# W2 block sums in the opening block, a reordered seam of the MLP products, and the last four tiles by column halves

## The reference

```python
def _mlp(h, w1, b1, w2, b2):
    return jnp.square(jax.nn.relu(h @ w1 + b1)) @ w2 + b2
...
        pl = jnp.split(hl @ w_in[l] + b_in[l], PROJ_SPLITS, axis=-1)
        ...
        hl2 = _modulate(xl, mod_l[3], mod_l[4])
        xl = _layernorm(DEEPNORM_ALPHA * xl + mod_l[5] * _mlp(hl2, w_mlp1[l], b_mlp1[l], w_mlp2[l], b_mlp2[l]),
                        ln_post_g[l, 1], ln_post_b[l, 1])
```

## Time and profile before

| | us |
|---|---|
| median of 3 runs (lowest to highest) | 3223.57 (3222.33 to 3227.64) |
| the profiled execution's own time | 3226.03 |
| its span, first to last instruction | 3224.2 |
| TensorE busy | 2957.7 (92%) |
| VectorE busy | 1853.1 (57%) |
| ScalarE busy | 1033.3 (32%) |
| GpSimd busy | 482.0 (15%) |
| mean granted TensorE clock, share of full | 0.965 |

### The profile page before, as it was taken

One profiled execution on the slowest core, in us unless ns is written; L12 is line 12 of the kernel. 1 busy time (PEld: TensorE's weight loads), 2 busy tenths in 40 slices (PEclk: granted clock), 3 DMA queues, 4 the chain that ended last, 5 costly groups with the idle time before them and its releaser, 6 DMA issues.

```text
span 3224.2 us, 35999 instructions
## 1 busy us (share of the span) xinstructions
PE 2957.7 (92%) x13816; PEld 2428.7 (75%) x13816; DVE 1853.1 (57%) x2496; ACT 1033.3 (32%) x1676; POOL 482.0 (15%) x628
## 2 busy tenths in 40 slices
PE   6999999999996889989999798897999799989994
PEld 3888888888884678868788576775888688878883
DVE  5831133112222878857766766665777666687667
ACT  2421000111112555542112444444555433313330
POOL 0423011010101222202202200010111000060003
PEclk9999999999999999989999898898999899999997
DMA  6732233333334545448847666776888755545552
GB/s 227 250 116 82 76 104 121 114 113 106 127 112 154 176 132 177 135 140 236 230 158 245 233 203 199 209 249 216 252 266 262 251 211 189 189 160 212 194 184 98
DMA packets 332912, 573.01 MB, mean 178 GB/s; under 512 B 23731, under 2 KB 212419, under 8 KB 326726
## 3 DMA queue, kind: packets, MB, share of 16 engines
q1 hardware_dynamic: 256646, 330.00, 32.1%
q0 software_dynamic: 58128, 200.85, 18.6%
q10 hardware_dynamic: 17968, 39.85, 3.7%
HBM read 371.37 MB, written 199.24 MB: 177 GB/s over the span
## 4 chain that ended last, share of the span: by engine, by line
PE 46%; DMA 9%; DVE 7%; issue 3%; ACT 2%; POOL 1%; SPq 0%; ACTq 0%; DVEq 0%; POOLq 0%
PE mix_bank L1562 5%; PE mix_bank L1563 5%; PE mix_bank L1564 5%; PE mix_bank L1524 4%; PE mix_bank L1525 4%; PE mix_bank L1526 4%; PE mix_bank L2328 3%; DMA tail_cm<-scratch_xn 3%; PE mix_bank L2267 2%; PE mix_bank L130 2%; PE mix_bank L132 2%; PE mix_bank L131 2%; DMA scratch_xn<-tail_cm 1%; PE mix_bank L1469 1%; PE mix_bank L1470 1%
## 5 line engine op out<-in xcount | busy, mean ns | idle before, releaser
L1524 PE MATMUL mix_bank<-tail_oph,tail_wh 128*128 128x512 f32 x896 | 363.7, 406 | 80.8 <-DVE tail_e L1113 46.2
L130 PE MATMUL head_bank<-head_hTh,head_wh 128*128 128x512 f32 x1024 | 400.9, 392 | 3.1 <-DVE head_hTl L547 2.3
L131 PE MATMUL head_bank<-head_hTl,head_wh 128*128 128x512 f32 x1024 | 398.6, 389 | 0.0
L132 PE MATMUL head_bank<-head_hTh,head_wl 128*128 128x512 f32 x1024 | 398.5, 389 | 0.0
L1562 PE MATMUL mix_bank<-tail_oph,tail_ah 128*128 128x512 f32 x896 | 353.9, 395 | 36.9 <-DVE tail_sum L1183 14.7
L1525 PE MATMUL mix_bank<-tail_opl,tail_wh 128*128 128x512 f32 x896 | 360.2, 402 | 0.0
L1526 PE MATMUL mix_bank<-tail_oph,tail_wl 128*128 128x512 f32 x896 | 359.8, 402 | 0.0
L555 DVE CAST head_wh<-head_raw 128x1024 fp32r<-128x1024 f32 x64 | 44.6, 697 | 543.5 <-PE head_bank L132 414.5
L1563 PE MATMUL mix_bank<-tail_opl,tail_ah 128*128 128x512 f32 x896 | 352.6, 393 | 0.0
L1564 PE MATMUL mix_bank<-tail_oph,tail_al 128*128 128x512 f32 x896 | 352.4, 393 | 0.0
L309 ACT ACTIVATE head_stage<-head_bank,all_b_in_col 128x512 f32<-128x512 f32 (+1 forms) x136 | 91.4, 677 | 590.8 <-PE head_bank L132 567.3
(11 more groups left out here) (274 smaller groups left out, 5477.6 us busy)
## 6 DMA issues: line engine op xcount, KB each, us to landing
tail_a<-scratch_a SPq DMA_DIRECT2D x112, 512.0 KB, 3.2
head_raw<-in_w_in SPq DMA_DIRECT2D x64, 512.0 KB, 4.1
scratch_proj<-head_stage POOLq DMA_DIRECT2D x128, 256.0 KB, 2.7
tail_raw<-in_w SPq DMA_DIRECT2D x64, 512.0 KB, 5.8
scratch_a<-tail_e SPq DMA_DIRECT2D x128, 256.0 KB, 6.3
tail_op<-scratch_w2t SPq DMA_DIRECT2D x28, 1024.0 KB, 5.7
scratch_a<-tail_sm SPq DMA_DIRECT2D x96, 256.0 KB, 8.8
tail_op<-in_w SPq DMA_DIRECT2D x21, 1024.0 KB, 5.7
```

Of the source, the lines that this page charges most:

```text
L130: nc.tensor.matmul(out, wh, xh, start=(k == 0), stop=False)
L131: nc.tensor.matmul(out, wh, xl, start=False, stop=False)
L132: last = nc.tensor.matmul(out, wl, xh, start=False, stop=(k == k_tiles - 1))
L1524: nc.tensor.matmul(out[:], wh[p % 7][:, k, :], oph[i][:, k, :], start=(k == 0 and i in (0, 1, 3)), stop=False, skip_group_check=True)
```

## The change

1. The 16 W2 block sums move to the opening block: SP loads the blocks into the idle `x` behind the weight pieces r = 13, 15, ... 43, VectorE sums each behind the weights of piece r+1 (`block_sums`), SP stores it behind the load of piece r+1.
2. `MIX` is 8, so the side work of the up product is four h sums and 16 row pieces, one in each unit at (u,5), for u = 2 to 14 and 17 to 23, the h sums first.
3. At the MLP seam SP issues the loads of op0 and a0 one unit earlier, and a4 ahead of op5 and op6; the waits for W2 sums fall away. VectorE and ScalarE split op5 and op6 behind down turns 2 and 3, and `paired(31)` goes behind down turn 4, its four stores behind turn 5 (they were behind turn 1).
4. The last four tiles are completed by column halves (`half`, `variance` in place of `complete`, `statistics`), two halves ahead of the sums of turn (15,5); the four `result` passes stand together at the end.

```diff
+            return (r - MIX0) // 2 if r >= MIX0 and (r - MIX0) % 2 == 0 and (r - MIX0) // 2 < NMIX else None
...
+                q = block_job(r)
+                if q is not None:
+                    if q:
+                        sp.wait_ge(blk_out, 32 * q)
...
+                    for n in range(2):
+                        sp.dma_start(x[:, 0, :, n * 512:(n + 1) * 512],
+                                     d["w2"][q * 2 * P:(q + 1) * 2 * P, n * 512:(n + 1) * 512].rearrange("(i p) n -> p i n", p=P)).then_inc(ld_blk, 16)
+                q = block_job(r - 1)
+                if q is not None:
+                    dst = d["w2t"][q // 4, :, :, q % 4]
+                    sp.wait_ge(blk_s, 4 * q + 3)
+                    sp.dma_start(dst[0:2].rearrange("o p n -> p o n"), mct.rearrange("p (o n) -> p o n", o=2)).then_inc(blk_out, 16)
+                    sp.wait_ge(blk_s, 4 * q + 4)
+                    sp.dma_start(dst[2:4].rearrange("o p n -> p o n"), mcm[:, 512:1536].rearrange("p (o n) -> p o n", o=2)).then_inc(blk_out, 16)
...
+                dve.wait_ge(ld_blk, 32 * (q + 1))
+                nc.vector.tensor_tensor(t1, b12, b11, ALU.subtract).then_inc(blk_s, 1)
...
-    MIX = 8 + UH
+    MIX = 8
...
-    WORK = [("row", n) for n in range(NTILE)] + [("mix", q) for q in range(4, MIX)]
...
+    WORK = [("mix", q) for q in range(4, MIX)] + [("row", n) for n in range(NTILE)]
+    WORK_AT = dict(zip([(u, 5) for u in range(2, NU - 1) if u not in (UH - 1, UH)], WORK))
...
-                sp.wait_ge(*mix_out(11 + 4 * b))
...
             if r == 0:
                 sp.wait_ge(st_left, LEFT0 + 16 * NTILE)
-                sp.wait_ge(*mix_out(MIX - 1))
...
+            if u == NU - 2:
+                sp.wait_ge(up_s, up_at[u + 1, 0] + 1)
+                load_w2(0, 0)
+                load_a(0)
...
+        load_a(4)
         for i in (5, 6):
             sp.wait_ge(up_s, up_at[NU - 1, i] + 1)
             load_w2(0, i)
...
-            if p == 1:
+            if p == 5:
                 store_mixed(NU - 1)
-            if p == 3:
+            if p == 8:
...
-        paired(NU - 1)
-        low_op(2, 5)
-        low_op(2, 6)
         for p in range(2, len(down_order)):
             down_turn(p)
+            if p in (2, 3):
+                low_op(2, p + 3)
+            if p == 4:
+                paired(NU - 1)
+            if down_order[p] == (NV - 1, 4):
+                half(*finals(NV - 1)[2], 0)
+                half(*finals(NV - 1)[3], 0)
```

More of the change, by code:

```diff
@@ L557, in weights, with block_sums @@
                 nc.vector.tensor_tensor(wl[:, r % 2], raw[:, r % 2], wh[:, r % 2].bitcast(F32), ALU.subtract).then_inc(w_split, 1)
+            def block_sums(r):
+                q = block_job(r - 1)
+                if q is None:
+                    return
+                b11, b12, b21, b22 = (mcm[:, n * 512:(n + 1) * 512] for n in range(4))
+                t1, t2 = mct[:, 0:512], mct[:, 512:1024]
+                dve.wait_ge(ld_blk, 32 * (q + 1))
+                nc.vector.tensor_tensor(t1, b12, b11, ALU.subtract).then_inc(blk_s, 1)
+                dve.wait_ge(blk_s, 4 * q + 1)
+                nc.vector.tensor_tensor(b12, b22, b12, ALU.subtract).then_inc(blk_s, 1)
+                nc.vector.tensor_tensor(t2, b22, t1, ALU.subtract).then_inc(blk_s, 1)
+                dve.wait_ge(blk_s, 4 * q + 3)
+                nc.vector.tensor_tensor(b21, b21, t2, ALU.subtract).then_inc(blk_s, 1)
             def rows_out(job):
@@ L608, in _ @@
                 weights(n + 1)
+                block_sums(n + 1)
             dve.wait_ge(st_b, 32)
@@ L611, in _ @@
                 weights(NS1 + n + 1)
+                block_sums(NS1 + n + 1)
                 if n % 4 == 3:
@@ L722, in tail_programs @@
     stats, mv, std, rstd = (bx.sb("stats", [P, 2, 2, 6]), bx.sb("mv", [P, NT, 2]), bx.sb("t_std", [P, NT]), bx.sb("t_rstd", [P, NT]))
+    final = place("final_stats", [P, 4, 2, 6], 196)
     b1 = bx.sb("b1", [P, FF // P])
@@ L991, in sync @@
             if u == NU - 1:
-                load_a(0)
                 load_a(1)
-                for i in range(2):
-                    sp.wait_ge(up_s, up_at[u, i] + 1)
-                    load_w2(0, i)
+                sp.wait_ge(up_s, up_at[u, 1] + 1)
+                load_w2(0, 1)
             if u:
@@ L1183, in summed, with half, variance @@
                     nc.vector.tensor_tensor(dst, dst, b[:], ALU.add).then_inc(sum_s, 1)
-        def complete(f, t):
-            dve.wait_ge(sum_s, 2 * len(down_order) - (2 if t >= 4 else 0))
-            step.up(nc.vector.tensor_tensor(sums[t][:], sums[t][:], g["mod5"][:], ALU.mult))
+        def half(f, t, c):
+            r, cs = sums[t][:, c * 512:(c + 1) * 512], slice(c * 512, (c + 1) * 512)
+            i = (5, 4)[c] if t >= 4 else (3, 6)[c]
+            dve.wait_ge(sum_s, 2 * (down_at[NV - 1, i] + 1))
+            step.up(nc.vector.tensor_tensor(r, r, g["mod5"][:, cs], ALU.mult))
             step.wait(dve)
             dve.wait_ge(ld_left, 64 * (f // 4 + 2))
-            nc.vector.tensor_tensor(sums[t][:], sums[t][:], left[f % 4][:], ALU.add).then_inc(whole, 1)
+            step.up(nc.vector.tensor_tensor(r, r, left[f % 4][:, cs], ALU.add))
+            step.wait(dve)
+            step.up(nc.vector.bn_stats(final[:, f % 4, c, :], r))
+        def variance(f, t):
+            step.wait(dve)
+            nc.vector.bn_aggr(mv[:, t, :], final[:, f % 4].rearrange("p a b -> p (a b)")).then_inc(mv_s, 1)
         def statistics(f, t):
@@ L1635, in load_row @@
             if n == 0:
-                pool.wait_ge(*mix_out(2))
-                pool.wait_ge(z_s, NTILE)
-                for s in range(2):
-                    pool.wait_ge(st_hf[s], 16 * 4 * 4)
+                pool.wait_ge(*mix_out(MIX - 1))
                 pool.dma_start(cm[0][:, 1, :], d["res"][0, :].partition_broadcast(P)).then_inc(ld_cm[0], 16)
```

69 lines of the change are left out of this document (34 added, 35 removed).

## The result

The changed kernel takes 3168.81 us at the median (3165.75 to 3169.87, four runs), the kernel before 3224.66 in the runs beside it. The ratio is 0.9825, 95% interval 0.9808 to 0.9842: 56 us or 1.7% faster, where I forecast 94, and outside my range on its slow side. The profiled execution has a span of 3166.8 us, against 3224.2. In one kernel further down, one of four executions took 3777 us at a granted clock of 0.745, and it is left out of that kernel's numbers.

A forecast was written before the change was run, and what follows sets the result against it. TensorE, busy 92%, was taken as the bound, losing time to side-work round trips. 47 + 30 + 16 + 1.5 - 1 = 93.5 us off 3226.0 gives 3132.5, forecast as 3130 us against the runs' median; range 3110 to 3160.

The forecast's parts named there:

- The row pieces, minus 47: Up product, 1900 to 2080 us: one piece a unit fits its round trip, so 47 of 48.3 us lost come back.
- The opening block, plus 1: Opening block, tightest at r = 32 to 43: added W2 block sums cost 1 us, taking the short end of the round.
- my own formula: Opening block: six rounds each late by their excess over 16.3 us, VectorE's head start hiding the first 6 us.
- weights that wait behind a block: Opening block: sign that the prediction is wrong, if weights there wait behind a W2 block.
- In front of unit 16 and in the exchange, minus 30: Up product around unit 16: 15.1 us of W2 waits vanish and 15.2 us of the h operand exchange's loss go.
- The term for the exchange (25.2 down to 10): h operand exchange, 2200 to 2260 us: 10 us remain, 4 for transfers, 2 for VectorE, 4 for lower-clock matmuls.
- 2 for VectorE behind its lookahead of five turns: h operand exchange: 2 us of the remaining 10 us loss, for VectorE's seven extra low parts, 15.7 us of work.
- the exchange keeps its loss: Rival, chance 0.19: transfers are the whole limit, the exchange's 25.2 us and half the seam's 16 stay, 3153 us.
- The MLP seam, minus 16: MLP seam, 2520 to 2580 us: gaps before down(0) and down(4) shrink, 6 of 22.2 us left; range minus 8 to 21.
- the 7.1 us of VectorE's work: MLP seam before down(4): unit 31's pair sums, 2.65 us, and op5 and op6 low parts, 4.49 us, move behind the copy.
- The end, minus 1.5: Last four tiles: two half tiles fill VectorE's idle time before the last sums, 1.5 us gained, between 0 and 4.
- the opening block pays in part, 20 us: Rival, chance 0.06: the opening block costs 20 us, for a time of 3150 us.

The follow-up runs named there:

- the ten like openings: Ten profiles whose opening block is that of the changed kernel; they reach unit 1 at 1862 to 1876 us, 1869.7 on the mean.
- without the ten jobs: Changed kernel without the ten W2 block-sum jobs in the opening block's pair pieces, first block's sums read instead: 3149.4 us, one run.
- with both orders mended: Changed kernel with SyncE's block loads and stores one piece later and VectorE's row sums ahead of block sums: 3143.3 us; with two exchange moves added, 3139.2 us.
- three swaps and a shift by one piece: Changed kernel with blocks one piece later on SyncE, row sums before block sums, exchange sums before low parts, op2's load before pair stores: 3139.2 us.
- the kernel with small splits: Changed kernel with high and low parts of the h operands of units 16 to 31 made of only 128 of 2048 columns: 3152.9 us, one run.
- the kernel with the row sums first alone: Changed kernel with only VectorE's row sums put ahead of the block sums in the opening block, SyncE as it is: 3167.5 us, one run.

## Why the prediction was wrong

- **The row pieces, minus 47: right**, 48.2 measured, by the round trip named; putting two in a unit again costs 60.7 us.
- **The opening block, plus 1: this is the step that failed.** I weighed the block's own round (14 to 20.6 us against 16.3), as load, sums and store, and took it that the weights are late only if that round doesn't fit. What I left out is whom the block's steps stand in front of: SyncE takes its instructions in order, one load of weights is issued behind the block's load, which waits for the stores of the block before to land, and the next one behind the stores, which wait for sums that VectorE makes behind the split of the late weights. So the weights' landing is a part of the block's round. That round came out at 17.35 us, 1.1 too long, which by my own formula costs 6.3 us for six blocks, less the 6.2 us of head start; with the block's steps one piece later it is 16.4 us. I had named weights that wait behind a block as what would refute me, but priced a different mechanism; the order of both queues would have shown this one. Measured: 14.7 us in the pairs; 9.4 come back by moving SyncE's block steps, the last 5.3 with the row sums put first. The other 7 us up to unit 1 are partly spread. Against the mean of the ten like openings the kernel is 19.7 us behind at unit 1, so some 5 us have no cause found; in the three profiles without the ten jobs or with both orders mended (1852.5, 1846.2 and 1850.2 us at unit 1) they are gone too.
- **In front of unit 16 and in the exchange, minus 30: 16.2.** The 15.1 us of the W2 waits went. The term for the exchange (25.2 down to 10) failed: 23.9 us stay. That is all that the sum missed there. Its size rested on bytes over 258 GB/s, a mean with idle slices, and on "2 for VectorE behind its lookahead of five turns". Shown in its place: a sum that TensorE waits for stands behind low parts that wait for ScalarE (9.6 us by changing that order alone); with the splits gone 16.7 us vanish, with the transfers gone 4.0. So my rival "the exchange keeps its loss" came true in its size and not by its cause, the transfers.
- **The MLP seam, minus 16: 15.3, with its causes misread in part.** About 6 of it are a by-product of the first part of the change and not of the moved loads. Of the other gap I gave the 7.1 us of VectorE's work that stood ahead of the copy to the moved pair sums and parts; they were worth 4.6, and the earlier loads the rest. So the size was right in part by luck.
- **The end, minus 1.5: the halves gave 2.5**, and 2.9 us came in behind the last store. They are in GpSimd's closing DRAIN, 7.57 us in place of 4.47; its cause is open, and the store's landing and three unused semaphores are excluded.
- Of the rivals "the opening block pays in part, 20 us" and "the exchange keeps its loss" both came true, together, at 0.06 and 0.19. My range left the two added up out.

## What to carry to other kernels

When work moves into an idle stretch, price not only its own round trip but what it is put in front of: for each in-order queue, ask which load was issued ahead before and is now behind a wait on another engine. An engine's waits tell quickly whether it is still ahead: `weights` waited for TensorE before and for its own load after. And where a short step that the bottleneck waits for stands behind a long one that waits for a third engine, swap them before counting bytes: three swaps and a shift by one piece, with no work less, gave 30 us.

## What the runs showed of the hardware that I had not expected

- From unit 14 to 17 the DMA engines moved 281 GB/s at a busy share of 0.87 in the kernel with small splits, against 224 at 0.71 in the changed kernel. So the mean of such a stretch is no limit of the engines. The highest mean over 20 us in the changed kernel is this:

```profile
2540.00:2560.00 20.00, 20.00 (x90) 16.57 (x89) 11.03 (x12) 7.72 (x6) 1.23 (x3) 1.00 1.02 400
```

  The Trainium skill, "DMA: Bandwidth & Descriptors", Specifications, puts the limit of HBM for a core at about 358 GB/s; the 400 GB/s of this row are above it, with the kernel on one core.
- Gaps cost more than their length: in the kernel with the row sums first alone, with four gaps of 2.2 to 5.0 us in the pairs, the 816 matmuls of the pairs are busy for 193.4 us at a mean granted clock of 0.96, against 185.2 us at 1.00.
- Twice the traffic in the opening block (205 against 107 GB/s in the pairs) cost TensorE nothing once the orders were right.
